# Delta-rule inverse: the work beside each width put in one place instead of two

## The reference

```
kk = einsum(k_beta, k) * seg
a_mat = eye + where(strict, kk, 0)
sol = triangular_solve(a_mat, [v_beta, k_beta * exp(b)])   # u, w
attn = einsum(q, k) * seg
v_new = u - w @ S;  o = q_dec @ S + attn @ v_new
S = S * exp(b_last) + k_out^T @ v_new
y = (rms_norm(o) * silu(z)) @ w_out
```

## Time and profile before

| | |
|---|---|
| median of three runs (2432.96 to 2438.77) | 2435.92 us |
| the profiled execution's own time | 2436.91 us |
| its span | 2435.1 us |
| PE busy over the span | 2303.9 us (95%) |
| DVE, ACT, POOL busy | 1497.9, 940.9, 870.6 us |
| granted TensorE clock, mean | 0.975 |
| one tile of the last phase (1968.18 to 2010.67) | 42.49 us |

### The profile page before, as it was taken

One profiled execution on the slowest core, in us unless ns is written; L12 is line 12 of the kernel. 1 busy time (PEld: TensorE's weight loads), 2 busy tenths in 40 slices (PEclk: granted clock), 3 DMA queues, 4 the chain that ended last, 5 costly groups with the idle time before them and its releaser, 6 DMA issues. The chain is left out here.

```text
span 2435.1 us, 54588 instructions
## 1 busy us (share of the span) xinstructions
PE 2303.9 (95%) x21003; PEld 1623.7 (67%) x21020; DVE 1497.9 (62%) x3167; ACT 940.9 (39%) x2596; POOL 870.6 (36%) x1090
## 2 busy tenths in 40 slices
PE   6999999999799997799999999996999999999997
PEld 2444444444556653588888888786787887878785
DVE  3343647561578765578576784565666676767665
ACT  3544444434111212444443543434444444444431
POOL 1552322323111111122222220116756566665652
PEclk8999999999899999899999999997999999999998
DMA  9453675855464445786766767546523231322213
GB/s 311 136 180 106 211 222 164 240 159 179 145 233 151 157 141 179 240 301 225 217 216 191 217 208 221 164 132 172 149 89 97 71 115 63 100 85 88 80 41 91
DMA packets 372150, 394.99 MB, mean 162 GB/s; under 512 B 39599, under 2 KB 263023, under 8 KB 371938
## 3 DMA queue, kind: packets, MB, share of 16 engines
q1 hardware_dynamic: 337826, 360.28, 47.1%
q10 hardware_dynamic: 34112, 31.71, 4.2%
HBM read 275.19 MB, written 116.72 MB: 161 GB/s over the span
## 5 line engine op out<-in xcount | busy, mean ns | idle before, releaser
L2792 DVE SCALAR_TENSOR_TENSOR inc_acc<-inc_ub,inc_taps,inc_acc 128x512 f32<-128x512 f32 x288 | 245.4, 852 | 11.0 <-ACT inc_acc L2632 4.2
L758 PE MATMUL inab_b<-inab_wt,keep 128*128 128x512 f16 x768 | 166.7, 379 | 1.6 <-POOL inab_wt L575 1.6
L758 PE MATMUL inab_b<-inab_wt,raw_next 128*128 128x512 f16 x768 | 166.4, 379 | 0.0
L2569 POOL COPY inc_halo<-inc_ub 128x3 f32<-128x3 f32 x96 | 49.0, 510 | 315.1 <-DVE inc_ub L2780 180.7
L1390 PE MATMUL mixab_y<-keep,mixab_oT_hi 128*128 128x512 f16 x512 | 153.1, 381 | 7.4 <-DVE mixab_f_y L1470 5.7
L739 POOL TENSOR_TENSOR inab_a_out<-inab_stage,inab_a_out 128x384 f16<-128x384 f32 x64 | 65.8, 1027 | 212.5 <-ACT inab_a_out L730 212.5
L758 PEld LDWEIGHTS inab_b<-inab_wt,keep 128*128 128x128 bf16 (+1 forms) x768 | 75.1, 98 | 91.1 <-issue 1.9
L758 PEld LDWEIGHTS inab_b<-inab_wt,raw_next 128*128 128x128 bf16 (+1 forms) x768 | 75.1, 98 | 89.9
L2636 ACT ACTIVATE inc_acc<-inc_acc 128x512 f32<-128x512 f32 x96 | 60.5, 630 | 141.6 <-DVE inc_acc L2792 141.4
L3607 DVE STREAM_TRANSPOSE mixc_N<-mixc_T 128x256 f32<-128x256 f32 (+1 forms) x130 | 57.9, 445 | 92.1 <-ACT mixc_T L3432 92.1
L2908 PE MATMUL inc_b<-inc_room,keep 128*128 128x256 bf16 (+3 forms) x864 | 109.3, 279 | 2.7 <-DVE stage_next L2762 2.7
(11 more groups left out here) (625 smaller groups left out, 6058.7 us busy)
## 6 DMA issues: line engine op xcount, KB each, us to landing
keep<-tmp_w SPq DMA_DIRECT2D x336, 256.0 KB, 3.3
tmp_qkv<-inc_acc SPq DMA_DIRECT2D x96, 256.0 KB, 2.8
inab_stage<-in_w_in_c SPq DMA_DIRECT2D x128, 128.0 KB, 2.6
tmp_w<-inab_stage SPq DMA_DIRECT2D x64, 256.0 KB, 3.2
inab_stage<-in_w_in_ab ACTq DMA_DIRECT2D x24, 512.0 KB, 4.1
tmp_w<-inab_a_out SPq DMA_DIRECT2D x64, 192.0 KB, 2.6
stage_next<-in_w_ada ACTq DMA_DIRECT2D x6, 2048.0 KB, 15.1
raw_next<-tmp_qkv SPq DMA_DIRECT2D x8, 1536.0 KB, 6.8
```

The source lines that it names most:

```text
L758: last = nc.tensor.matmul(dst, lhs(a, k), rhs(b, k), start=(k == 0 and i == 0), stop=(k == KT - 1 and i == len(PASSES) - 1))
L2569: pool.tensor_copy(halo[:, g, :], ub[w % 2][side][:, BLK:]).then_inc(halo_saved[side], 1)
L2792: ins = dve.scalar_tensor_tensor(a_v, u_[:, i:i + BLK], taps[:, g, i:i + 1], a_v, ALU.mult, ALU.add)
```

## The change

Part 0 of `beside` does nothing any more, and part 1 does the work of both. For k = 0 and 1 two heads of the projection (6 products) stand after `y(k,1)` (for k = 0 after `tn(0,0)`), for k = 2 and 3 all four heads of the query-key products (4 products, 8 records) after `y(k,1)`. No instruction is added or removed, and only PE's order changes; the orders of DVE, ACT, POOL and of the queues are the same. What is waited for by which step is the same too.

```diff
@@ -3973,11 +3973,13 @@
             half, n2 = (t + 1) // 2, P if t + 1 < nt else NS
 
             def beside(k, part):
+                if part == 0:
+                    return
                 if k < 2 and t >= 2:
-                    fin.project(pe, t - 2, P, 1, [4 + 2 * k + part])
+                    fin.project(pe, t - 2, P, 1, [4 + 2 * k, 5 + 2 * k])
                 if k in (2, 3):
-                    query_keys(t, par, P, k - 2, QK[k - 2], (part,))
-                if k == 4 and part == 1:
+                    query_keys(t, par, P, k - 2, QK[k - 2])
+                if k == 4:
                     turn_k(t + 1, nxt, half, n2, 1)
 
             levels(t, BOTH, LEVELS, beside)
```

## The result

The changed kernel takes 2439.67 us, the median of 22 runs (2434.93 to 2446.23); the kernel before, on the same chip, 2437.58 us (2430.7 to 2443.95, 22 runs). The ratio is 1.0016, 95% interval 1.0008 to 1.0023: 3.9 us slower by the ratio, 2.1 by the medians. The forecast was 2427.3 us, 8.6 us faster, and the range ended at 2434. It was wrong in its sign.

The account below looks back on a forecast made before the run. PE's instruction list was taken to bound each tile; 0.56 us less in 14 tiles (7.8) and 0.38 in tiles 0 and 1 (0.8) gave 8.6 us, from 2435.9 to 2427.3. Ends 2423.7 to 2430.3; 8-in-10 range 2421 to 2434.

Parts of the forecast that it names:

- What bounds the kernel, and the gain between two starts: PE's instruction list sets the tile's time; each place beside the inverse costs 0.15 or 0.24 us beyond its products.
- Width 0: Period of k = 0: from 3.20 to 3.11 us, 0.09 less, with tn(0,0) 1.11 us after y(0,0).
- the wait is longer at the first width: Rival at k = 0: y(0,0) to tn(0,0) takes 0.35 us more than 1.11; gain 3.7, 2432.2 us; chance 0.14.
- Widths 1 to 3: Periods: k = 1 from 3.66 to 3.57 us, 0.09 less; k = 2 from 3.44 to 3.25, 0.19 less; k = 3 likewise.
- the doubled work: Query-key products at k = 2 and 3: 0.64 us for four records with the way out, plus 4 x 0.112.
- the way from y(k,1) into the full-size work: From the last small step to the larger products: 0.57 us to the projection at k = 1, 0.56 to the query-key products.
- the whole drain is saved: Rival: each merged place saves 0.33 us, less 0.06 for the wait; 1.08 per tile, 2419.7 us; chance 0.06.
- merging saves nothing: Rival: the extra time belongs to each product, only waits are left, +0.06 x 60 = 3.6; 2439.5 us; chance 0.08.
- PE runs out of instructions: Rival: longer runs of small products outrun instruction supply, 1.33 us once in each later tile; +10.0, 2445.9 us; chance 0.06.
- The DMA engines are idle around the inverse: Argument against stalls: in the steady state they carry only three fetches in the 20 us around the inverse.
- The last width already has four small steps in a row without a gap: Argument against stalls: that run, its third step twice as long, shows no gap beyond 1.13 us.
- The row that was read as the sign: Tile 1, behind eight small steps: tn(1,1) started only at 1720.42, after 1.33 us of PE idle time.

Follow-up runs that it names:

- e16: The kernel before with every query-key product computed twice, still in the order before; 2467.37 us, ratio 1.0124 to before.
- e15: The changed kernel with every query-key product computed twice; 2460.26 us, ratio 1.0096 to before.
- e5: The changed kernel with PE's wait for `q_sq` moved ahead of y(0,0); ratio 1.0015 to before.
- e2: The kernel before with only the query-key products at widths 2 and 3 merged; ratio 0.9986 to before, 3.4 us faster.
- e7: Only the query-key products at widths 2 and 3 merged, plus 32 semaphore increments ahead of tile 0; ratio 1.0019 to before, 4.6 us slower.
- e14: The changed kernel without the query-key products of heads 0 and 2 of each group at widths 2 and 3 from tile 2 on; 2440.87 us, ratio 1.0013.
- e8: The changed kernel with width 0 left unmerged, so only widths 1, 2 and 3 merged; ratio 1.0015 to before.
- e9: The changed kernel without three of four query-key products at each of widths 2 and 3 from tile 2 on; ratio 1.0022 to before.

## Why the prediction was wrong, step by step

**What bounds the kernel, and the gain between two starts:** right. The 0.15 and 0.24 us per place out of the small size and back are real; e16 and e15 show the net 0.15 at widths 2 and 3 on its own.

**Width 0 (−0.09 forecast, +0.10 measured):** this term of the sum was mis-sized. The 1.11 us from y(k,0) to tn(k,0), read at width 1 of tile 1, was taken for width 0 too, which has a second semaphore instruction on PE's queue; it is 1.27 us there, and another 0.02 to 0.03 is lost on the way into the projection. The rival "the wait is longer at the first width" had the place, with 0.35 us and DVE as its cause; measured are 0.16 us and PE's own queue (e5).

**Widths 1 to 3 (−0.09, −0.19, −0.19; measured −0.06, −0.15, −0.15):** tn(k,0) at 1.12 and y(k,1) at 1.60 came as forecast, and the doubled work too (1986.14 to 1987.23 is 1.09 us, as 0.64 + 4 x 0.112). What was mis-sized is the way from y(k,1) into the full-size work: 0.60 us where a wait stands in the run, taken as 0.56 to 0.57. With width 0 this makes 0.27 instead of 0.56 per tile and 4.4 instead of 8.6 us in all.

**The rivals on the drain:** "the whole drain is saved" wanted 0.27 us per place (0.33 less 0.06) and "merging saves nothing" a loss of 0.06; the periods show 0.15 won at widths 2 and 3 and 0.06 at width 1, so neither holds.

**"PE runs out of instructions" (chance 0.06):** this is the step that turned the sign. The sum put the supply of instructions at nothing; this rival is what happened, and both arguments against it were wrong. *The DMA engines are idle around the inverse*: they are after, too (the same stretch has q8 at 0.8%), but the fetch starts late all the same, up to 4.6 us after PE began the block before, with the DMA engines idle until then. *The last width already has four small steps in a row without a gap*: a gap shows only where a block's end falls into such a stretch and the fetch is late; one tile without it says nothing of the next. The row that was read as the sign, 1.33 us ahead of tn(1,1) in tile 1, was indeed such a gap: it stands at the same number modulo 256, and the fetch landed at 1718.74, 1.6 us before PE went on. The price, 1.33 in each tile, was wrong in shape: some tiles have nothing, others up to 1.7 us and the fallen clock on top. And it was said to decide from 0.6 us per tile on; with the true gain it decides from 0.27 (4.4 us over 16 tiles).

**The balance:** −4.4 by the periods and +3.9 by the ratio leave 8.3 us for the supply of instructions on the mean of the runs. This is a difference, not a measurement; measured are the 11.7 us of tiles 2 to 15 in the one profiled execution, half of them through the clock, and how often the clock falls in the other executions is not known.

**What stays open:** why the fetches start later in the merged order. The trace has the start of a fetch on its DMA queue, not the request for it, and no run here shows PE's sequencer. Nor was a complete kernel found that keeps the merging and has no gaps: e2 has four short ones and is 0.14% faster than before; the same with the blocks' ends shifted by 32 (e7) has five and is 0.19% slower, so the gain of e2 may be luck of where the ends fall.

## What to carry to other kernels

An order that packs small products closer together does not only shift work; here it used instructions faster, and a stream that had just been fast enough became the bound, though the other engines and the DMA looked free. Before such a change, look for a step broken in two with "issue" behind it, count the instructions from one such break to the next, and see how much time the densest block leaves. And read a wait's length at the very step it will stand at, with the semaphore instructions ahead of it, not at its neighbour.

## What the runs showed of the hardware

- PE's instructions came in blocks of 256; a fetch took 0.9 to 1.5 us, and PE went on 1.2 to 1.6 us after it had landed. Gaps stood behind blocks used up in 5.0 to 6.9 us.
- A gap of 1.7 us could bring the clock from 2.4 to 1.2 GHz for some 10 us (tile 4 of the changed kernel, from 1.4 us after PE went on) or 3.4 us (tile 2), together about 6 us, as much as all six gaps. One of 1.45 us in e14 did it too. Not each one did: two of 1.4 and 1.5 us in e8 and one of 1.8 in e9 left it at 2.4.
- Less work need not take less time: with 18.7 us less, e9 was no faster than the changed kernel.
- An increment of a semaphore by PE's queue took 0.15 us, and a second wait in a row ahead of a waited step cost 0.17 us per tile (3.30 against 3.13 in e5).
